# Moving half of the embedding's projection into the transposition of x that stands ahead of its gate

## The reference, cut to what matters

```
h = h + concat(hm, ha) @ w_out                            # 1536 -> 1024
h = h + (p @ w_ple) * sigmoid(h @ w_ple_gate)             # p: 256 x 256, the embedding
x = rmsnorm(h, norm_final)
```

## Time and profile before

| | |
|---|---|
| median of three runs | 880.56 us |
| the profiled execution's own time | 880.37 us |
| its span (first to last instruction) | 878.6 us |
| TensorE matmul busy | 854.5 us (97%) |
| VectorE busy | 666.8 us (76%) |
| ScalarE busy | 457.9 us (52%) |
| GpSimd busy | 70.1 us (8%) |
| mean granted TensorE clock | 0.998 |
| DMA | 200.67 MB, mean 228 GB/s |

### The profile page before, as it was taken

The page is one execution under the profiler, slowest core; times in us unless marked ns, Lnnn a source line. Parts: engine busy times, 40 slices in busy tenths (PEclk is TensorE's granted clock), DMA queues, the critical chain, the costliest instruction groups (busy, mean ns, idle before and its releaser), DMA issues. The chain is left out here.

```text
span 878.6 us, 14632 instructions
## 1 busy us (share of the span) xinstructions
PE 854.5 (97%) x5810; PEld 751.8 (86%) x5810; DVE 666.8 (76%) x1096; ACT 457.9 (52%) x737; POOL 70.1 (8%) x61
## 2 busy tenths in 40 slices
PE   9999999999999999999999999999999999999996
PEld 8989987777876987699999999689977899999995
DVE  6698796888887988799658757797777876566567
ACT  5564554554456545475454454365563854454450
POOL 1100001000001120012201000110000101001011
PEclk9999999999999999999999999999999999999999
DMA  9856664566775861989748795379627876646501
GB/s 345 299 182 219 200 216 154 193 202 242 270 296 221 290 223 29 405 315 361 279 152 269 273 392 189 105 272 351 216 72 297 315 298 200 210 150 198 186 1 48
DMA packets 56916, 200.67 MB, mean 228 GB/s; under 512 B 6600, under 2 KB 7936, under 8 KB 56848
## 3 DMA queue, kind: packets, MB, share of 16 engines
q1 hardware_dynamic: 55808, 196.50, 63.5%
q0 software_dynamic: 1040, 3.24, 1.2%
HBM read 198.57 MB, written 1.08 MB: 227 GB/s over the span
## 5 line engine op out<-in xcount | busy, mean ns | idle before, releaser
L1279 PE MATMUL ps<-XT,wsp 128*128 128x256 f32 x760 | 215.0, 283 | 2.1 <-issue 1.6
L1280 PE MATMUL ps<-XT,wsp 128*128 128x256 f32 x760 | 212.1, 279 | 0.0
L1281 PE MATMUL ps<-XT,wsp 128*128 128x256 f32 x760 | 211.9, 279 | 0.0
L1520 DVE TENSOR_TENSOR wsp<-ring,wsp 128x1024 fp32r<-128x1024 f32 x136 | 165.9, 1228 | 8.2 <-ACT wsp L2096 8.2
L2096 ACT CAST wsp<-ring 128x1024 fp32r<-128x1024 f32 x136 | 141.3, 1046 | 56.9 <-PE ps L1281 48.6
L1279 PEld LDWEIGHTS ps<-XT,wsp 128*128 128x128 f32 x760 | 142.7, 188 | 5.5 <-issue 3.6
L1280 PEld LDWEIGHTS ps<-XT,wsp 128*128 128x128 f32 x760 | 142.6, 188 | 0.5
L1281 PEld LDWEIGHTS ps<-XT,wsp 128*128 128x128 f32 x760 | 142.5, 188 | 0.0
L1279 PE MATMUL ps<-wsp,ra 128*128 128x512 f32 (+1 forms) x256 | 97.8, 382 | 3.9 <-DVE ra L1835 2.1
L1281 PE MATMUL ps<-wsp,ra 128*128 128x512 f32 (+1 forms) x256 | 97.0, 379 | 0.0
L1280 PE MATMUL ps<-wsp,ra 128*128 128x512 f32 (+1 forms) x256 | 96.6, 377 | 0.0
(11 more groups left out here) (279 smaller groups left out, 1534.2 us busy)
## 6 DMA issues: line engine op xcount, KB each, us to landing
ring<-in_mod_w SPq DMA_DIRECT2D x47, 512.0 KB, 4.6
arena<-in_mod_w SPq DMA_DIRECT2D x46, 512.0 KB, 6.4
ring<-in_ffn_o SPq DMA_DIRECT2D x27, 512.0 KB, 4.8
ring<-in_ffn_a SPq DMA_DIRECT2D x26, 512.0 KB, 5.3
ring<-in_ffn_b SPq DMA_DIRECT2D x26, 512.0 KB, 5.0
arena<-in_ffn_b SPq DMA_DIRECT2D x18, 512.0 KB, 4.9
arena<-in_ffn_a SPq DMA_DIRECT2D x18, 512.0 KB, 4.9
arena<-in_ffn_o SPq DMA_DIRECT2D x17, 512.0 KB, 4.8
```

The lines of the kernel that those rows point to most:

```text
L1279: pe.matmul(o, l[0], r[0], start=start, stop=False)
L1280: pe.matmul(o, l[0], r[1], start=False, stop=False)
L1281: return pe.matmul(o, l[1], r[0], start=False, stop=stop)
L1520: ve.tensor_tensor(w[:, 1024:1024 + n], raw[slot[0]][:, 0:n], w[:, 0:n].bitcast(f32), SUB).then_inc(*done("V", "lo", u, also=[("raw", *slo ...
```

## The change

The units are taken in another order (w_ple's second tile behind w_out's last), the two `row` steps of that tile stand inside the transposition of x, one behind the eight transpositions of each half of the rows, and the fifth part is allowed only after it.

```diff
-    plan("w_ple", 2)
+    plan("w_ple", 1)
     units.extend(("w_out", u, 1024) for u in range(6, 12))
+    units.append(("w_ple", 1, 1024))
@@
-    proj_a("pt2", 2, "w_ple", 0, 2, lambda t, cb, b: add("ev_ple", t, cb, b))
+    proj_a("pt2", 2, "w_ple", 0, 1, lambda t, cb, b: add("ev_ple", t, 0, b))
@@
     add("kr_zero")
-    more_part(("ple", 1, 1))
     tbl = W.beside(tables(), 1.0)
@@
     mod[0][1], tbl[1] = MOD_PACE[0], 1.0
-    transposed("x1", 8, None, apart=True)
+    b1 = [bank.get(), bank.get()]
+    got = [W.next("w_ple", 1)]
+
+    def ple(t):
+        add("row", "pt2", 2, got, 0, t, b1[t], prior("bank", b1[t]), True)
+        add("ev_ple", t, 1, b1[t])
+        bank.put(b1[t][0])
+
+    transposed("x1", 8, None, apart=True, filled=(lambda: ple(0), lambda: ple(1)))
+    W.done(got[0][1])
+    more_part(("ple", 1, 1))
```

## The result

The changed kernel takes 886.27 us (median of six runs, 885.67 to 887.05) against 880.51 us (six runs): ratio 1.0066, 95% interval 1.0056 to 1.0076, so 5.8 us slower. Its profiled execution took 886.63 us, with a span of 884.8 us and a mean granted clock of 0.994 (before 878.6 us and 0.998). The busy time of VectorE and ScalarE is what it was; TensorE's is 856.7 us instead of 854.5.

A forecast was written before the change was run, and what follows sets the result against it. TensorE bounds the kernel (matmuls fill 97% of the span), plus gaps in its stream. -0.67 + 1.05 + 4.3 = +4.7 us on the profiled 880.37, taken as 885.2 us at the median; range 882.9 to 888.4.

The forecast's parts named there:

- Part a: Transposition of x before the gate: moved tile halves fill TensorE's 0.79 us gap; gain 0.67 us, bounds -0.8 to +0.4.
- the first rival: End of MLA: the clock falls in TensorE's new wait, up to +4.85 us, halfway +2.4, 887.6 us; chance 0.18.
- The edge at the gate's third unit: In the gate: VectorE's `lo` for the third unit ends just when needed; 0 to 0.4 us lost.
- Part b: w_out with four parts instead of five: TensorE waits 1.05 us for the last unit's `lo`; bounds 0 to 1.4.
- Part c: End of MLA: `mod_sum` behind `ln_fin` holds up `mod_pe` and TensorE; net +4.3 us, bounds +3.4 to +4.9.
- The row that was to give the rival its chance: Kernel's last 4.6 us, without any matmul: mean granted clock 0.62, read as a fall to 1.2 GHz.
- Shorter than the wait that lost it: End of MLA: argument against the clock's fall, that the new wait is shorter than the last window's.
- The chain is not late: End of MLA: `mod_sum` not behind `ln_fin` or covered, so c is 0; 880.9 us, or 879.9; chance 0.15.
- only the gap goes: Ahead of the gate: at most 0.79 us gained, everything else hidden, 879.7 us; chance 0.05.
- the layer norm's own wait gives cover: End of MLA: 0.82 us of idle at the same transpositions spoke for some cover of the late chain.

The follow-up runs named there:

- the kernel with one advance less: Kernel before, with only the modulation turned off one unit of the gate earlier, so five tiles there and not six; 885.16 us, ratio 1.0052.
- the fifth part taken away: Kernel before, with the fifth part allowed only behind the transposition of x, w_ple's second tile left where it was; 886.86 us, ratio 1.0068.
- the advance put back: Changed kernel with the refused modulation advance made in the gate: limit 4.2, 882.03 us; limit 4.7 with tables turned off earlier, 882.78 us.
- the wait ahead of the layer norm's last part: Changed kernel with until(0, 4) ahead of ln_fin of rows 128 to 255, so mod_sum precedes its two activations on ScalarE; 881.99 us, ratio 1.0025.
- the ready matmuls first: Changed kernel with the five mod_k tiles ahead of mod_one and of the wait at the end of MLA; 882.82 us, ratio 1.0027.
- the tables later: Changed kernel with the missing advance back (limit 4.7) and the tables turned off one unit earlier in w_out; 882.78 us, ratio 1.0024.

## Why the prediction was right, point by point

It gave 885.2 us, slower, and the time is 886.3. The order of the steps came out as derived: five tiles ahead of the end of the gate, `mod_one` behind MLA's last matmul and `mod_sum` behind `ln_fin`. What did not hold is a condition of the forecast, that the clock stays up. That the number is only 1.1 us low is in part luck: the fall of the clock cost 2.3 us, and MLA's 0.65 and 0.4 of part a, which it did not have, gave 1.0 back. The mechanism that happened is that of the first rival, which was put at 887.6 us.

**Part a** was put at -0.67 (-0.8 to +0.4; its own terms, 5.59 less 4.9, give -0.69). From the transpositions' start to the gate it takes 243.63 - 239.08 = 4.55 us and not 4.9; with the tile's 2.89 that stretch was 5.59, so -1.0. Two groups of eight transpositions start 0.79 us ahead of what follows them (239.08 to 239.87, 241.36 to 242.15), not half of sixteen's 1.91, which counts to the end of the last one (a group of eight takes 1.03 by that count). The outer bound was too narrow. The edge at the gate's third unit cost nothing; the gate as a whole took 0.21 more (0.60 behind, then 0.81).

**Part b**, +1.05 us. Start to start, 239.08 - 0.53 against 240.33 - 2.89: +1.1. Right: 0.75 shows as a wait, and with the slower starts around it (233.63, 234.77 and 235.11 us, where the others are 0.23 apart) it is 1.0. Taken together with a, the two cancel up to the gate.

**Part c**, +4.3 us, is the term that was mis-sized, at 6.4. Its wait was right: 4.46 us of idle against 4.6, and 4.1 net. What was missing is the clock, 2.3 us. That was a rival with a chance of 0.18, at +2.4. The sentence of the Trainium skill, TensorE: Matmul & The Clock Gate, Part 1: The HAM clock gate, that idleness halves the array's clock and sustained activity brings it back, agrees with the trace: 0.59 in the stretch of the wait, 0.50 behind it, 1.00 from 374 us on.

The row that was to give the rival its chance, was misread. Its 4.6 us are not TensorE's idle time, which begins earlier. The last matmul of the kernel before, and its stretches of half a microsecond:

```profile
...
870.49 0.28 PE L1281 MATMUL ps<-ra 128*128 128x256 f32 x1
```

```profile
...
874.50:875.00 0.50, 0.00 (x0) 0.00 (x0) 0.50 (x2) 0.00 (x0) 0.04 (x1) 1.00 0.00 0
875.00:875.50 0.50, 0.00 (x0) 0.00 (x0) 0.50 (x2) 0.00 (x0) 0.00 (x0) 0.62 0.00 0
...
```

There TensorE had done nothing for 4.2 us and the granted clock was still at its upper level. In the change it began to fall between 366.0 and 366.5 us, with no matmul since 364.04; in the kernel with one advance less between 365.0 and 365.5 (none since 362.02), in that with the fifth part taken away between 367.5 and 368.0 (none since 363.92). So the fall came after 2.0 to 4.7 us of idle, at another point each time, and no row of before could settle whether a wait of 4.5 us would keep the clock. "Shorter than the wait that lost it" was no argument against the fall. Behind all three waits of this length that were profiled it had fallen.

**The rivals.** "The chain is not late" and "only the gap goes" fell with the first trace. That the layer norm's own wait gives cover was wrong: with the clock held up the loss stays at 4.1.

**Not foreseen:** MLA's 0.65 us. I had looked for a cost of the shifted `mod_v` there and found none; that the shift takes one away, the wait of 0.49 at 321.38 us for `pb`, was not looked for. That wait is there in the two kernels with the advance put back (0.48 in each) and in none of those with five tiles; the other 0.16 were not traced. In all: a and b and the gate +0.3, MLA -0.65, c +6.4 make 6.05, for 5.8 by the medians.

## What to carry to other kernels

Where one list orders the instructions of several engines, a move is paid where the list changes, not where the edit is: derive the new order up to the next point that forces something, and ask at that point which engine's queue the forced step joins. A side task that is late by one step costs nothing until a waiting instruction stands behind a long chain on one engine and ahead of ready work on another; moving the ready work or the forced step won most of the loss back here (882.8 and 882.0 us), and making the side task in time won all of it (880.3). And count a wait of several microseconds on TensorE twice, once for itself and once for the clock behind it, here 4.1 and 2.3 us.

## What the runs showed of the hardware

In the profiled executions waits of 2.16, 2.30 and 2.83 us (the kernels with the wait ahead of the layer norm's last part, the ready matmuls first, the tables later) left the granted clock at its upper level. One of 4.45 or 4.46 us lost it in each of the three profiled kernels that had it with nothing in it, and the 40 small matmuls behind it took 4.34 to 4.50 us instead of 2.37. How long TensorE had been idle when the clock fell differed: between 2.0 and 2.5 us in the change, over 4.2 us at the end of the kernel before. Executions of one and the same kernel with a wait of 2.16, 2.30 or 2.83 us lie 1.8 to 2.4 us apart, the longer ones mostly at a lower mean clock (0.995 to 0.997 against 0.997 to 0.999); those of each of the five kernels of the experiments in which TensorE waits 1.66 us at the longest lie within 1.3 us, at 0.997 to 0.999.

Matmuls whose result is thrown away, put into the wait, were enough to keep the clock up (1.00 throughout). Eight transpositions between other matmuls took 0.79 us from their start to the next start and 1.03 to the end of the last; sixteen in a row ahead of an idle stretch took 1.91 to the end of the last.
